# First projection by k tiles in six PSUM banks, scale columns multiplied on TensorE, products of ones between the first sums

## What is computed

```python
c_act = silu(c)                                    # [1, 1024]
mod = c_act @ ada_w[layer] + ada_b[layer]          # 1024 x 6144
sh_m, sc_m, g_m, sh_f, sc_f, g_f = split(mod, 6)
h = rms_norm(x, pre_mix_g[layer]) * (1 + sc_m) + sh_m
z = gelu(h @ w_in + b_in)                          # 1024 x 4096
u, v = split(z, 2)
v = layer_norm(v, ln_g, ln_b)                      # over 2048
v = einsum('gts,bnsgc->bntgc', tril(w_s), v) + b_s # 16 groups of 128
y = (u * v) @ w_out
```

## Time and profile before

| what | value |
|---|---|
| median of 3 runs | 1818.83 us (1813.96 to 1819.66) |
| the profiled execution | 1818.1 us, its span 1816.3 us |
| TensorE busy | 1728.5 us, 95% |
| VectorE busy | 1165.3 us, 64% |
| ScalarE busy | 897.2 us, 49% |
| moved | 363.43 MB, mean 200 GB/s |

### The profile page before, as it was taken

One profiled execution on the slowest core, in us unless ns is written; L12 is line 12 of the kernel. 1 busy time (PEld: TensorE's weight loads), 2 busy tenths in 40 slices (PEclk: granted clock), 3 DMA queues, 4 the chain that ended last, 5 costly groups with the idle time before them and its releaser, 6 DMA issues.

```text
span 1816.3 us, 22000 instructions
## 1 busy us (share of the span) xinstructions
PE 1728.5 (95%) x8926; PEld 1439.5 (79%) x8926; DVE 1165.3 (64%) x1604; ACT 897.2 (49%) x1251; POOL 7.4 (0%) x20
## 2 busy tenths in 40 slices
PE   3999999999997999999999979999999999999998
PEld 2798787879765888888889856888888889778887
DVE  6888788786666854465546884655565546675553
ACT  3445543467655544454435546544454445574442
POOL 0000000000000000000000000000000000000000
PEclk7999999999989999999999979999999999999999
DMA  9768487864325664555455412554555456335451
GB/s 393 289 261 324 163 348 300 343 267 167 138 94 231 230 228 170 200 203 186 168 203 188 149 47 104 204 179 174 210 196 180 170 197 251 107 135 191 174 196 47
DMA packets 54117, 363.43 MB, mean 200 GB/s; under 512 B 5744, under 2 KB 8944, under 8 KB 13056
## 3 DMA queue, kind: packets, MB, share of 16 engines
q1 hardware_dynamic: 52256, 351.47, 52.7%
q0 software_dynamic: 1760, 10.56, 1.5%
HBM read 360.95 MB, written 1.05 MB: 199 GB/s over the span
## 4 chain that ended last, share of the span: by engine, by line
PE 85%; DVE 8%; ACT 3%; DMA 3%; issue 1%; SPq 0%; ACTq 0%; DVEq 0%
PE pp L597 81%; DMA raw<-in_w 3%; DVE low L1725 2%; PE pp L847 2%; DVE raw L1738 2%; PE pp L779 1%; ACT wh L1252 1%; DVE hf L1869 1%; PE pp L923 1%; DVE x L1728 0%; DVE tb L1725 0%; ACT junk L1285 0%; ACT Pb L1485 0%; DVE hl L1725 0%; ACT PT L1494 0%
## 5 line engine op out<-in xcount | busy, mean ns | idle before, releaser
L1725 DVE TENSOR_TENSOR low<-raw,wh 128x2048 fp32r<-128x2048 f32 (+3 forms) x337 | 637.1, 1906 | 372.2 <-ACT wh L1252 372.0
L1252 ACT ACTIVATE wh<-raw 128x2048 fp32r<-128x2048 f32 (+3 forms) x337 | 534.6, 1604 | 433.6 <-PE pp L597 313.4
L597 PE MATMUL pp<-wh,hh 128*128 128x512 f32 x1312 | 523.5, 399 | 25.6 <-ACT wh L1252 21.1
L597 PE MATMUL pp<-low,hh 128*128 128x512 f32 x1312 | 515.0, 393 | 3.3 <-DVE low L1725 3.1
L597 PE MATMUL pp<-wh,hl 128*128 128x512 f32 x1312 | 508.1, 392 | 3.8 <-DVE hl L1725 3.7
L597 PEld LDWEIGHTS pp<-wh,hh 128*128 128x128 f32 x1312 | 248.6, 190 | 82.8 <-ACT wh L1252 21.9
L597 PEld LDWEIGHTS pp<-wh,hl 128*128 128x128 f32 x1312 | 248.0, 189 | 58.1 <-DVE hl L1725 5.8
L597 PEld LDWEIGHTS pp<-low,hh 128*128 128x128 f32 x1312 | 248.8, 190 | 54.9 <-DVE low L1725 5.1
L597 PE MATMUL pp<-wh,hidh 128*128 128x512 f32 x592 | 232.1, 392 | 0.0
L597 PE MATMUL pp<-low,hidh 128*128 128x512 f32 x592 | 230.7, 390 | 0.0
L597 PE MATMUL pp<-wh,hidl 128*128 128x512 f32 x592 | 230.6, 390 | 0.0
(11 more groups left out here) (200 smaller groups left out, 1185.0 us busy)
## 6 DMA issues: line engine op xcount, KB each, us to landing
raw<-in_w SPq DMA_DIRECT2D x314, 1024.0 KB, 4.8
raw<-in_w SPq DMA_DIRECT2D x24, 768.0 KB, 4.3
gain<-in_w POOLq DMA_DIRECT2D x6, 512.0 KB, 4.9
bT<-in_rel POOLq DMA_DIRECT2D x1, 2048.0 KB, 12.2
cst<-in_csts POOLq DMA_DIRECT2D x1, 1029.0 KB, 9.5
xT<-in_xT SPq DMA_DIRECT2D x1, 1024.0 KB, 6.6
wsT<-in_ws POOLq DMA_DIRECT2D x1, 1024.0 KB, 13.7
binr<-in_bin POOLq DMA_DIRECT2D x1, 1024.0 KB, 16.9
```

What stands on the lines that cost most here:

```text
L597: return e.matmul(out, lhsT, rhs, start=start, stop=stop, skip_group_check=True)
L1252: q.then_inc(e.activation(wh[j % NW][:, c], raw[i % NRAW][:, c], ACT.Copy), s_wh, (j, part))
L1725: return e.tensor_tensor(out, a, b, op)
```

## The change

1. `a_v` 0 to 2 become one group of 1536 columns, with one k tile to an item (0.75 MiB), eight items. Their sums stand in six banks, the three pairs, and for each k tile all 18 products are done. `a_v` 3 keeps its two pieces and takes the two `misc` banks.
2. Ada pieces 4 to 7 become items of kind `col`: TensorE multiplies them, 16 fp32 products of 128x128 weights by one column of `ccol` (silu(c) on partitions, a new load with 4-byte runs that is the first in SyncE's queue), and VectorE only adds the bias. The stream begins ada 0, col 4, k tiles 0 and 1, ada 1, col 5, k tiles 2 and 3, ada 2, col 6, k tiles 4 and 5, ada 8, ada 3, col 7, k tiles 6 and 7, ada 9, ada 10, the pieces of `a_v` 3. `marks` follow.
3. TensorE does 16, 6 and 10 products of ones by ones (fp32, 128 columns) before the squares, before the first columns and after them.
4. x comes in two halves, ahead of `col`.
5. The bias additions of `a_v` 0 to 2 come after the low parts of all of `a_v`; the ones products of `spatial_bias` move into and behind `a_u` 1; v is normalised on ScalarE (scale and bias in one instruction) instead of VectorE; the tri mask moves ahead.

```diff
-    add("a_v", "a_w_in", (0,), 8, split(2048, 4))
+    add("a_v", "a_w_in", (0,), 8, split(3584, 1), 3)
...
-    items = [ada[4], ada[0], ada[5], ada[1], main[0], ada[6], ada[2], ada[7], ada[3], main[1]]
-    ada, main = ada[8:], main[2:]
-
-    marks = [(0, 0), (4, 0), (18, 12), (26, 12), (46, 28), (54, 36), (72, 36), (76, 44), (82, 44), (92, 48)]
+    first = [("mm", [("a_w_in", (0,), cols(2048, 1536))], k, 1, 1536, ("a_v", 0)) for k in range(8)]
+    items = []
+    for i in range(4):
+        items += [ada[i], ("col", *ada[4 + i][1:]), first[2 * i], first[2 * i + 1]]
+        items += {2: ada[8:9], 3: ada[9:11]}.get(i, [])
+    ada = ada[11:]
+
+    marks = [(0, 0), (2, 0), (14, 9), (22, 9), (42, 25), (50, 33), (68, 33), (72, 41), (78, 41), (88, 45)]
...
+            def idle(n):
+
+                for _ in range(n):
+                    mm(outs[2, 1][:, 0:128], ones, ones, True, True)
+
+            def columns(i):
+
+                c = items[i][6]
+                b, before = misc.begin(("col", c), (s_mod, ("mod", c)))
+                if before:
+                    q.wait_ge(*before)
+                q.wait_ge(s_cact, "columns")
+                q.wait_ge(s_raw[i % NRAW], i // NRAW)
+                w = raw[i % NRAW][:, :].rearrange("p (k n) -> p k n", k=8)
+                for m in range(2):
+                    for k in range(8):
+                        ins = mm(b[:, m:m + 1], w[:, k, 128 * m:128 * m + 128], ccol[:, k:k + 1], m == 0 and k == 0, k == 7)
+                q.then_inc(ins, s_col, i)
+
+            def first_products(j, k, g, m):
+
+                w_h, w_l, k0, kt, n = weights(j)
+                at, c, t = k0 + k, slice(512 * g, 512 * g + 512) if n > 512 else slice(0, 512), slice(128 * m, 128 * m + 128)
+                q.wait_ge(s_wh, j)
+                q.wait_ge(s_hi, ("h", 0, at, m))
+                mm(outs[g, m], hh[:, at, t], w_h[:, k, c], at == 0, False)
+                q.wait_ge(s_lo, ("h", 0, at, m))
+                mm(outs[g, m], hl[:, at, t], w_h[:, k, c], False, False)
+                q.wait_ge(s_wl, j)
+                return mm(outs[g, m], hh[:, at, t], w_l[:, k, c], False, at == 7)
+
+            q.wait_ge(s_set, "ones")
+            idle(16)
             stats("x0")
-            rows("a_v", 0, h(0), (s_side, ("a_v", 0)))
-            rows("a_v", 1, h(0), (s_side, ("a_v", 1)))
+            idle(6)
+            scales = [i for i, it in enumerate(items) if it[0] == "col"]
+            columns(scales[0])
+            idle(10)
+            for j in of_group[("a_v", 0)]:
+                for g in range(3):
+                    for m in range(2):
+                        ins = first_products(j, 0, g, m)
...
+                if j in (0, 2, 4):
+                    columns(scales[1 + j // 2])
...
-            rows("a_v", 2, h(0), (s_side, ("a_v", 2)), between=lambda: spatial_bias(0))
-            rows("a_v", 3, h(0), (s_side, ("a_v", 3)), between=lambda: spatial_bias(1))
-            for g in range(2):
-                whole("a_u", g, h(0), (s_gate, ("a_u", g)))
+            whole("a_u", 0, h(0), (s_gate, ("a_u", 0)))
+            whole("a_u", 1, h(0), (s_gate, ("a_u", 1)), between=lambda: spatial_bias(0))
+            spatial_bias(1)
...
+                if items[i][0] == "col":
+                    c = items[i][6]
+                    q.wait_ge(s_col, i)
+                    q.wait_ge(s_ld["col"], 0)
+                    q.then_inc(tt(mod[:, 2 * c:2 * c + 2], misc.of(("col", c))[:, 0:2],
+                                  col[:, COL["ada_b"] + 2 * c:COL["ada_b"] + 2 * c + 2], ALU.add), s_mod, ("mod", c))
...
+            for g in range(3):
+                with_bias(g)
+            for g in range(3):
+                v_sums(g)
+            ahead.upto(11)
+            with_bias(3)
+            ahead.upto(12)
+            v_sums(3)
...
+            q.then_inc(stt(less_mean, mv[:, :, 0], -1.0, rstd, ALU.mult, ALU.mult), s_side, "less_mean")
+            ahead.upto(14)
+            spatial_bias(0)
+            spatial_bias(1)
             ahead.group("a_u", 1)
...
+            e.dma_start(ccol[:, :], c_d.rearrange("(k p) -> p k", p=128), allow_slow_non_contiguous=True).then_inc(s_ld["ccol"].sem, 16)
```

More of the change, by code:

```diff
@@ new lines, in tensor_program @@
+            for m in range(2):
+                outs[3, m], before = misc.begin(("a_v3", m), (s_side, ("a_v", 3)))
+                q.wait_ge(*before)
+            ja, jb = of_group[("a_v", 3)]
+            for k in range(4):
+                for m in range(2):
+                    ins = first_products(ja, k, 3, m)
+            q.then_inc(ins, s_mm, ("piece", ja))
+            for m in range(2):
+                for k in range(4):
+                    ins = first_products(jb, k, 3, m)
+                q.then_inc(ins, s_mm, ("a_v", 3, m))
@@ L1035, in spatial_bias @@
+            s_mm.at["piece", jb] = s_mm.n
             def spatial_bias(g):
@@ L1235, in taken @@
         def taken(i):
-            return (s_mm, ("piece", order[i])) if items[i][0] == "mm" else (s_ada, i)
+            return {"mm": (s_mm, ("piece", order.get(i))), "ada": (s_ada, i), "col": (s_col, i)}[items[i][0]]
         def scalar_program(e):
@@ L1592, in scalar_program @@
             first_root()
-            first_h(range(0, 4))
+            for i in range(4):
+                ahead.upto(2 * i)
+                first_h((2 * i, 2 * i + 1))
+                ahead.upto(2 * i + 1)
+            ahead.upto(10)
             def gelu_v(g):
@@ L2204, in first_h @@
                 first_h_of(j, der[:, 0, :], (s_side, ("der0", j)))
-            def second_half():
-                while ahead.item < 9:
+            for i in range(4):
+                ahead.rest()
+                if i == 0:
+                    q.wait_ge(s_root, "x0")
+                    q.then_inc(e.reciprocal(rsx[:, :], root[:, :]), s_rs, "x0")
+                ahead.rest()
+                first_h(i)
+                ahead.rest()
+                ahead.rest()
+                if i == 2:
                     ahead.rest()
[L2209 to L2213, removed]
+                    q.wait_ge(s_ld["ws"], 0)
+                    q.wait_ge(s_ld["cst"], 0)
+                    q.then_inc(tt(wsT[:, :, :], wsT[:, :, :], bc4(tri[:, :], 16), ALU.mult), s_side, "tri")
+            ahead.upto(9)
             def spatial_bias(g):
@@ L2223, in spatial_bias, with with_bias, v_sums @@
                     q.then_inc(ins, s_side, ("bias", n))
-            for g in range(4):
-                ahead.group("a_v", g, between=second_half if g == 0 else (lambda: spatial_bias(g - 2)) if g >= 2 else None,
-                            ahead=1 if g == 0 else NW)
+            q.wait_ge(s_ld["bin"], 0)
+            def with_bias(g):
                 s, before = tb.begin(("a_v", g), (s_sideact, ("gelu_v", g)))
                 q.wait_ge(*before)
[L2230 to L2237, removed]
+                for m in range(2):
+                    q.wait_ge(s_mm, ("a_v", g, m))
+                    b = pairs.of(("a_v", g)).rows[:, m, :] if g < 3 else misc.of(("a_v3", m))[:, :]
+                    ins = tt(tokens2(s)[:, m, :], b, binr[:, 512 * g:512 * g + 512], ALU.add)
+                q.then_inc(ins, s_side, ("a_v", g))
+            def v_sums(g):
                 q.wait_ge(s_sideact, ("gelu_v", g))
```

52 lines of the change are left out of this document (32 added, 20 removed).

## The result

After: 1828.62 us (median of 6 runs, 1825.61 to 1833.27). Before, in the same comparison: 1818.95 us (6 runs). The ratio is 1.0060 with a 95% interval of 1.0042 to 1.0078: slower by 9.7 us at the medians, where 5.7 were forecast, and inside the range of 1813.5 to 1831. The profiled execution of the changed kernel took 1829.6 us, 11.5 us more than that of before.

The account below looks back on a forecast made before the run. TensorE, busy 95% of the span, bounds the kernel, with VectorE's arrival at `spt` the last link of the front. Arrival +3.2 and clock +2.5 made +5.7 us on the median 1818.83: 1824.5 us, range 1813.5 to 1831.

Parts of the forecast that it names:

- The likeliest case: VectorE reaches `spt` late, TensorE stalls 6.7 us at the fourth spatial product, then loses clock: 1824.5 us, chance 0.45.
- the root and a cast: VectorE's wait for these between 56.6 us and `spt`: 1.3 us.
- The cost of the clock behind the stall: After the fourth spatial product's stall, about 5 us of TensorE work at half clock: 2.5 us lost.
- item 18: VectorE waits 0.9 us for this transfer, whose slot opens when TensorE is through k tile 5 (64.5).
- `a_v` 3's first piece: VectorE waits 2.0 us for this transfer, landing at 72.0, with a cast of 1.9.
- rival 2: Clock lost earlier: TensorE stands 4.0 us before `col7`, 1.2 GHz then delays item 18's slot; +8.7, 1829 us; chance 0.2.
- the ones products of `bias` 2: VectorE waits 2.0 us for these before `spt`, as they now stand behind all of `a_u` 1.
- cost nothing by themselves: VectorE's waits behind column sets (3.0, 3.6, 4.3 us) are covered by waits for item 12's landing and `col7`.
- nothing changed after `a_out`: Behind the front nothing changes: ada pieces given out by mid-`a_out` stay 20, and no TensorE wait can absorb the shift.
- `ccol`: Load of 1,024 runs of 4 bytes, first in SyncE's queue, delays all behind it: 2.0 us, bounds 0 and 4.0.
- Case 3: About level: `ccol` near its lower bound, no clock lost, a shorter column: 1819.5 us, chance 0.2.
- case 4: Faster: TensorE sets the time, VectorE's waits after 56.6 vanish, `sp` starts at 108: -7, 1812 us; chance 0.15.

Follow-up runs that it names:

- half-column run: Changed kernel, each column set multiplying only k tiles 0 to 3 of its ada piece, 16 instructions in place of 32: 1823.22 us.
- ada 8 later: Changed kernel with ada piece 8 behind k tile 7 in the stream instead of ahead of ada 3 and the last column piece: 1826.48 us.
- without ones: Changed kernel with the 32 products of ones left out: 1822.88 us.
- scales on VectorE: Changed kernel with the four scale pieces as ada pieces on VectorE again, TensorE's columns gone: 1820.14 us.
- both combined ones: Changed kernel, scale pieces on VectorE, a_u 1's items before second bsb additions: 1817.65 us; also ada piece 8 behind k tile 7, no ones products: 1815.15.
- `ccol` run: Changed kernel with ccol loaded from contiguous rows of 32 bytes, 128 runs instead of 1,024: 1829.38 us.
- columns set earlier: Changed kernel with the second column set directly behind the first, replacing ten products of ones, and the third behind k tile 1: 1836.87 us.
- bias pieces around ada work: Changed kernel with VectorE's items ahead for a_u 1 done before the second bsb additions instead of behind them: 1825.82 us.

## Why the prediction was right, and what was off by 4 us

**Right.** The likeliest case came about: `spt` on VectorE ends the front, TensorE waits 6.98 us there (forecast 6.7) and works at 1.2 GHz behind it. A column set took 3.63 us (3.7); `col7` landed at 57.05 (56.6); the sets end at 61.2 (60.4). VectorE's work from there was summed at 57.2; measured, 129.71 less 61.20 is 68.5, and less the waits of 9.9 and about 0.8 of starts it is 57.8. ScalarE's `v` pass took 4.09 us (3.8); it did delay one cast, and the low part behind it by 1.28, which the forecast had in its 1.3 for "the root and a cast" (the root added 0.36). The cost of the clock behind the stall was 2.5 forecast; from 131.34 to 135.5 TensorE worked for 4.2 us at half speed, 2.1 lost. By the profiled executions the forecast was off by more than the medians say: +5.7 was forecast and +11.5 measured, and 5.5 of the 5.8 us between them arose up to `spt`.

**Mis-sized: item 18.** The step that failed is "0.9 for item 18, whose slot opens when TensorE is through k tile 5 (64.5); 2.0 for `a_v` 3's first piece (lands 72.0 ...)". TensorE was through k tile 5 at 66.7. Of the 2.2 us, 0.5 are `col7`'s later landing, and most of the rest is the clock, which was at 1.2 GHz for 3.4 us from 60.5, between the last columns and the first products of k tile 5. That is rival 2's consequence ("item 18's slot opens that much later and both of VectorE's waits for that queue ... grow with it") without its cause: TensorE stood for 0.99 us before `col7` and not for 4.0. The queue behind it moved on only then: `a_v` 3's first piece took 8.21 us from issue to landing, and landed at 75.31. Waits: 2.10 and 3.24 in place of 0.9 and 2.0. The wait for the ones products of `bias` 2 was 3.27 for 2.0, because TensorE was late by the same cause (`a_v` ended at 92.39, not 87.2: its last piece began 3.5 us late, and the rest is the stretch at 1.2 GHz up to 84.3). These are 3.7 us of waits; with the columns' 0.8 and about 1 of starts and small work they make the arrival 129.71 instead of 124.2. Both engines slipped by the same 5 us, and the stall between them kept its forecast length. That was no luck of two errors: VectorE waits for TensorE's ones products there, so it can't slip alone.

**Wrong: columns that "cost nothing by themselves".** The forecast looked at VectorE's waits of 3.0, 3.6 and 4.3 (measured 2.55, 4.33, 5.84) and took them as covered, because VectorE would wait at 49.7 for item 12 and then for `col7`. That cover did not come: the 2.34 us idle before 49.62 were ended by ScalarE's `hh`, VectorE never waited for item 12, and it came to the fourth add with a wait of 0.17 us. So 12.7 us of waits stand against 9.9 of saved work. The forecast also missed what stands behind the columns on the other engine. On TensorE the fourth set is ahead of k tile 5, waits for a landing and holds k tile 5's buffer with it.

That the columns are what costs is shown both ways: without them 8 us came back, and the DMA engines' 425 GB/s; put into before, they cost 11. Through which of their effects is shown less well. The buffer of k tile 5 accounts for the arrival at `spt` in the traces, where halving the products moved nothing; but halving them, with the order kept, brought the time down as far as taking them away, and with it the time at 1.2 GHz. That a plain reordering, the fourth set behind k tile 5, would help was not tried.

**Wrong: "nothing changed after `a_out`".** The profiled difference is 8.65 at `spt`, 10.3 near 200 us and still 10.3 when TensorE reaches the wait for VectorE near 300 us. That wait is 3.33 where before waited 1.96, and behind it comes a stretch at 1.2 GHz from 306.2 to 313.0 (the window above): by VectorE's instructions, counted from the program's end, the difference is 14.3 at 315 us. It is 11.5 at the end, as both have further stretches later, and before spends some 7 us more in them. The same 20 us in before have the clock at 1.00 throughout, as they do in the half-column run:

```profile
300.00:320.00 20.00, 18.56 (x86) 15.09 (x85) 16.77 (x23) 9.94 (x8) 0.00 (x0) 1.00 0.87 333
```

It is full too in the profiled executions with ada 8 later, without ones, with scales on VectorE and in both combined ones, and partly lost (0.91) in the first two and the `ccol` run (and 0.93 and 0.91 in before with `v` on ScalarE and with columns); but it is full in the slowest kernel too, that with a columns set earlier. What goes with it is TensorE's wait there. It was 3.05 to 3.34 us in after and the three of its versions that lost clock, and 1.35 to 2.34 in the seven that did not, and 1.96 in before; yet 2.00 and 2.07 in the two versions of before that lost some too. Each has one profiled execution, so this is a pattern and no proof; it fits that leaving out ones, or half of the columns, shortens the time by 5 to 6 us without moving `spt`. Why VectorE comes later to this place in some runs, and what decides whether the clock falls, stays open.

**`ccol`.** It was charged 2.0; the first item landed 1.6 us later than before, of which 0.6 may be the form of the load. What of it stood on the path is small: the chain of after starts with `cact`, which landed 5.0 us after its issue instead of 4.0, and the squares start at 9.19 instead of 8.86. With contiguous rows the time was the same. The Trainium skill (DMA: Bandwidth & Descriptors, Rules for kernel authors) says that such a load becomes one descriptor per element; this trace agrees. The view of DMA for the first 12 us, before, then after:

```profile
DMA packets 1590, 3.75 MB, mean 313 GB/s; under 512 B 65, under 2 KB 1217, under 8 KB 1345
```
```profile
DMA packets 2584, 3.26 MB, mean 271 GB/s; under 512 B 1120, under 2 KB 2272, under 8 KB 2400
```

That is 1,055 more small packets for a vector of 1,024 numbers, and 0.49 MB less moved, 1.2 us at 421 GB/s. With contiguous rows there were 224 under 512 B, 896 fewer, which is 1,024 runs less 128.

**The rivals.** Case 3 (level) fell with the stall, case 4 (faster) because VectorE never came near 115; its idea that filling TensorE's early idle helps gets no support: leaving the ones out made the run shorter. Case 2's time, 1829, is the nearest to the median, its mechanism being half of what happened. That the likeliest case misses the medians by 4 us only, and the profiled executions by 5.8, is luck: before's was 0.9 us below its median and after's 0.9 above.

## What to carry to other kernels

When work moves to an engine with idle time, ask what stands behind it in that engine's order, and which buffers that work gives back: here a 4 us job that waits for a landing held a buffer, and the DMA engines all but stood for 5 us. Compare its price with what it relieves: here 9.9 us of VectorE's work were bought with 12.7 us of VectorE's waits. An engine that waits in order for one late transfer makes the next one late. A stall that an edit removes is worth nothing until the engine that was late is less late: moving `spt` forward took away 7.0 us of waiting and gave 4.8 back 20 us later, with no certain gain in time. And a stall that has the same length in every version (6.98 us in seven) is made by an order of one engine that waits for the other, not by two engines that happen to arrive apart.

## What was not expected of the hardware

- A product with one column costs as much as its weight load: 3.63 us for 32 instructions of 128x128 fp32 weights, 0.113 each, beside 3.77 us in which their weight loads were busy; and 6.95 at 1.2 GHz.
- TensorE may be busy throughout and its granted clock still be 0.50: 29.7 to 36.5 in the changed kernel, with 6.80 of 6.80 us busy. Nor did products of ones in its idle time keep the clock up: up to 68 us the changed kernel was at 1.2 GHz for 20.4 us with them and for 20.5 without. In the changed kernel each of the four falls between 15 and 68 us (near 19.5, 29.7, 46.8 and 60.5) comes in the course of a column set or less than 1 us behind one.
- The length of a stall doesn't settle what the clock does. At the fourth spatial product, 6.98 us were followed by 1.2 GHz, as were 4.74 and 3.57 in the two combined kernels, and 3.19 (bias pieces around ada work) and 2.00 (before) by full clock; but 2.00 and 2.01 in the two versions of before were followed by 1.2 GHz too, and the 16 products took 2.92 and 3.21 us instead of 2.05.
- Executions of one kernel differ by 4 to 9 us, and one profiled execution can lie 4.6 us from its median; the arrival at `spt` and the medians rank these kernels differently.
